# Gates: the weighted one-hot columns of eight tokens are shared between VectorE, GpSimd and ScalarE

## The reference

```python
s, i = lax.top_k(scores, PEER_TOPK)                  # 16 of 128 keys, two halves, 8 heads
cand_s = s[..., 0, :, None] + s[..., 1, None, :]
top_s, sel = lax.top_k(cand_s, PEER_TOPK)            # 16 of 256 pairs
idx = take_along_axis(i0 * 128 + i1, sel)            # one of 16384 experts
gate = softmax(top_s)
act = gelu(einsum('td,ted->te', hx, peer_u[idx]))
out = einsum('te,ted->td', gate * act, peer_v[idx])
```

## Time and profile before

| | us |
|---|---|
| median of 3 runs | 4343.73 (4340.94 to 4347.49) |
| the profiled execution | 4342.6 |
| its span | 4340.8 |
| TensorE busy in the span | 4061.2 |
| VectorE busy | 3090.5 |
| ScalarE busy | 2417.5 |
| GpSimd busy | 95.5 |

### The profile page before, as it was taken

How to read it: one execution, slowest core, us unless ns; L and a number is a source line. 1 busy time by engine, 2 the same in 40 slices (tenths; PEclk the granted TensorE clock), 3 DMA queues, 4 the chain that set the end, 5 groups by cost and what they waited for, 6 DMA issues and landing times.

```text
span 4340.8 us, 84350 instructions
## 1 busy us (share of the span) xinstructions
PE 4061.2 (94%) x30146; PEld 3730.5 (86%) x30146; DVE 3090.5 (71%) x5150; ACT 2417.5 (56%) x4061; POOL 95.5 (2%) x182
## 2 busy tenths in 40 slices
PE   6999997899999999789998999969998999987999
PEld 6899997788889999778888999968887899986887
DVE  6758858867565886787766688598776578768555
ACT  4156658544534665754456666574444466566444
POOL 0000000000000000000000000001000000000000
PEclk9999999999998999999998999999998899999999
DMA  8345551678513555257853555418882255532554
GB/s 283 104 146 175 179 183 54 217 246 289 174 51 127 175 178 181 75 180 250 285 179 120 167 178 180 155 47 298 284 288 106 93 167 176 179 121 68 193 193 155
DMA packets 203625, 748.66 MB, mean 172 GB/s; under 512 B 22704, under 2 KB 23856, under 8 KB 202192
## 3 DMA queue, kind: packets, MB, share of 16 engines
q1 hardware_dynamic: 178416, 646.51, 44.4%
q0 software_dynamic: 25056, 100.15, 7.5%
HBM read 745.52 MB, written 1.05 MB: 172 GB/s over the span
## 4 chain that ended last, share of the span: by engine, by line
PE 83%; DVE 10%; issue 3%; ACT 3%; DMA 1%; DVEq 1%; SPq 0%; ACTq 0%
PE ps L1925 15%; PE ps L1926 14%; PE ps L1932 14%; PE ps L2368 11%; PE ps L2371 11%; PE ps L2375 11%; DVE t_lo L1766 3%; PE ps L2073 2%; DVE arena L1785 2%; DVE oh L1774 2%; PE ps L1946 1%; ACT t_hi L632 1%; DMA raw<-w_tiles 1%; PE ps L2326 1%; PE ps L2217 1%
## 5 line engine op out<-in xcount | busy, mean ns | idle before, releaser
L1108 DVE TENSOR_TENSOR t_lo<-raw,t_hi 128x1024 fp32r<-128x1024 f32 x1180 | 1445.8, 1226 | 1038.2 <-ACT t_hi L632 1017.6
L632 ACT CAST t_hi<-raw 128x1024 fp32r<-128x1024 f32 x1180 | 1237.9, 1050 | 1527.5 <-PE ps L1932 755.5
L1925 PE MATMUL ps<-h_hi,t_hi 128*128 128x256 f32 x5344 | 1349.6, 289 | 42.6 <-DVE h_lo L1240 20.3
L1926 PE MATMUL ps<-h_lo,t_hi 128*128 128x256 f32 x5344 | 1327.6, 285 | 0.0
L1925 PEld LDWEIGHTS ps<-h_hi,t_hi 128*128 128x128 f32 x5344 | 1035.4, 194 | 66.8 <-issue 43.6
L1926 PEld LDWEIGHTS ps<-h_lo,t_hi 128*128 128x128 f32 x5344 | 1038.8, 194 | 0.8 <-issue 0.5
L1932 PE MATMUL ps<-h_hi,t_lo 128*128 128x256 f32 x5240 | 735.2, 283 | 0.0
L1932 PEld LDWEIGHTS ps<-h_hi,t_lo 128*128 128x128 f32 x5240 | 676.3, 192 | 0.0
L2368 PE MATMUL ps<-t_hi,h_hi 128*128 128x512 f32 x2048 | 548.8, 390 | 9.3 <-DVE h_lo L1816 9.3
L2371 PE MATMUL ps<-t_hi,h_lo 128*128 128x512 f32 x2048 | 549.2, 390 | 0.0
L2375 PE MATMUL ps<-t_lo,h_hi 128*128 128x512 f32 x2048 | 548.5, 390 | 0.0
(11 more groups left out here) (284 smaller groups left out, 2961.9 us busy)
## 6 DMA issues: line engine op xcount, KB each, us to landing
raw<-u_tiles SPq DMA_DIRECT2D x512, 512.0 KB, 3.3
raw<-v_tiles SPq DMA_DIRECT2D x512, 512.0 KB, 4.2
raw<-w_tiles SPq DMA_DIRECT2D x188, 512.0 KB, 3.6
oh<-w_tiles POOLq DMA_DIRECT2D x160, 512.0 KB, 4.8
arena<-w_tiles SPq DMA_DIRECT2D x16, 512.0 KB, 3.7
arena<-keys_t POOLq DMA_DIRECT2D x4, 1024.0 KB, 5.0
arena<-mla_w POOLq DMA_DIRECT2D x1, 4096.0 KB, 15.0
arena<-lora POOLq DMA_DIRECT2D x2, 1280.0 KB, 8.8
```

What stands on the lines that cost most here:

```text
L632: act.copy(t_hi[:, j % SPL, :], raw[:, j % RAW, :]).then_inc(hi_done, 1)
L1108: tts(t_lo[:, j % SPL, :], raw[:, j % RAW, :], t_hi[:, j % SPL, :].bitcast(F32), ALU.subtract).then_inc(lo_done, 1)
L1925: mm(o, hi[:, c, :], h_hi[:, c, :], start=(c == 0), stop=False)
L1926: mm(o, hi[:, c, :], h_lo[:, c, :], start=False, stop=False)
```

## The change

A third semaphore, `pooled`, and a function for GpSimd, `middle_hots`, are added. GpSimd makes the columns of tokens 2 and 3 of each octet with the same operation that VectorE uses; VectorE makes those of tokens 0 and 1 only; ScalarE's four stay as they are. TensorE does the products in three groups, 2, 2 and 4, with a wait ahead of each. The results are the same numbers in the same places.

```diff
--- before.py
+++ after.py
@@ -138,6 +138,7 @@
 HSPLIT = {"ffn0": 3, "ffn1": 6, "ffn2": 9, "ffn3": 13, "wo": 11}
 
 EB = 4
+POOL_FROM, POOL_TO = 2, 4
 GATE_BANKS = [6, 0]
 LRU_BANKS = [2, 4, 6, 2]
 POOL_BANKS = [6, 7, 2, 3]
@@ -502,6 +503,7 @@
         hot = sem("hot")
         away_done = sem("away_done")
         weighted = sem("weighted")
+        pooled = sem("pooled")
         gates_t = sem("gates_t")
         gated = sem("gated")
         wah = sem("wah")
@@ -586,6 +588,19 @@
                     tile = 8 * FOLD_ORDER[l][t // 8] + t % 8
                     pool.dma_start(fold_bufs[t % 2], w_tiles[first + tile]).then_inc(ada_in[t % 2], 16)
 
+            def middle_hots(l):
+
+                n = T // 8
+                pool.wait_ge(sel_ready, TT * (l + 1))
+                for m in range(n):
+                    if m >= 2:
+                        pool.wait_ge(gates_t, n * l + m - 1)
+                    for q in range(POOL_FROM, POOL_TO):
+                        t = 8 * m + q
+                        ins = pool.tensor_scalar(hot_cols[m % 2][:, q, :], iota, sel[:, 1, t:t + 1], sel[:, 2, t:t + 1],
+                                                 ALU.is_equal, ALU.mult)
+                    ins.then_inc(pooled, 1)
+
             for l in range(4):
                 if l:
                     if l == 2:
@@ -614,6 +629,7 @@
 
                 pool.wait_ge(h_split, DC * HSPLIT[f"ffn{l}"])
                 pool.dma_start(tk["keys"], keys_t[l]).then_inc(keys_in, 16)
+                middle_hots(l)
                 if l < 3:
                     fetch_late(l + 1)
 
@@ -1768,7 +1784,7 @@
 
                 def columns(m, b):
 
-                    for q in range(4):
+                    for q in range(POOL_FROM):
                         col = lambda w: sel[:, w, bass.ds(m * 8 + q, 1)] if not isinstance(m, int) \
                             else sel[:, w, 8 * m + q:8 * m + q + 1]
                         ins = ts(hot_cols[b][:, q, :], iota, col(1), col(2), ALU.is_equal, ALU.mult)
@@ -2340,18 +2356,19 @@
 
                 def gate(b):
 
-                    for half, made in enumerate((hot, weighted)):
+                    for made, qs in ((hot, range(POOL_FROM)), (pooled, range(POOL_FROM, POOL_TO)),
+                                     (weighted, range(POOL_TO, 8))):
                         seen(made)
-                        o = ps[:, GATE_BANKS[b] + half, :].rearrange("p (e t) -> p e t", t=4)
-                        for q in range(4):
-                            ins = mm(o[:, :, q], hot_rows(l, b)[:, 4 * half + q, :].bitcast(F32),
-                                     hot_cols[b][:, 4 * half + q, :], start=True, stop=True)
+                        for q in qs:
+                            o = ps[:, GATE_BANKS[b] + q // 4, :].rearrange("p (e t) -> p e t", t=4)
+                            ins = mm(o[:, :, q % 4], hot_rows(l, b)[:, q, :].bitcast(F32),
+                                     hot_cols[b][:, q, :], start=True, stop=True)
                     ins.then_inc(gates_t, 1)
 
                 gate(0)
                 pe.wait_ge(taken, TAKEN[f"u{l}"] + KEYS)
                 gate(1)
-                with seen.loop(T // 16 - 1, {hot: 2, weighted: 2, gated: 2}):
+                with seen.loop(T // 16 - 1, {hot: 2, pooled: 2, weighted: 2, gated: 2}):
                     for b in range(2):
                         seen(gated)
                         gate(b)
```

## The result

The changed kernel takes 4292.5 us (median of 4 runs, 4286.2 to 4295.5) against 4343.0 us before: a ratio of 0.9885, 95% interval 0.9874 to 0.9897, that is 50.5 us less. In a second session on one chip it took 4285.8 us against 4342.8, 0.9872 (0.9857 to 0.9887).

What follows compares the result with a forecast made beforehand. VectorE was taken to bound the gate stages at 3.29 us an octet, ScalarE next at 2.85. Four layers gain 45.3 us: 4342.6 - 45.3 = 4297.3, plus 1.1 to the median, 4298 us; range at 8 in 10, 4290 to 4385.

Steps and rivals of the forecast that it cites:

- VectorE bounds, a column is worth 0.255 us, ScalarE's 2.85 us is next: Gate loop: without two VectorE columns, the octet falls from 3.29 us to ScalarE's 2.85 us, not 2.78.
- The end of the stage: First layer's last octets: weights, cast, subtraction, then last gate at 775.5 instead of 786.85, 11.3 us gained.
- thirty cycles on: First layer: octet 31's weights start 30 x 2.853 us after octet 1's at 686.12, at 771.7.
- GpSimd's price: GpSimd's columns: 0.48 us each, 0.96 us a pair, with 0.20 and 1.61 us a pair as ends.
- What an overlap costs: Gate loop: where GpSimd's pair meets VectorE's rows or columns, VectorE would be held; beside the gate multiply it would not.
- A: Rival, gate loop: GpSimd starts between rows and columns, columns wait for the pair; cycle 3.74 us, total 4398; chance 0.24.
- B: Rival, gate loop: pair outlasts the gate multiply and holds the rows; at 0.70 us each, cycle 3.14, total 4326; chance 0.12.
- C: Rival, gate loop: GpSimd at its ceiling, 1.61 us a pair, holds the rows; cycle 3.35 us, 4351 or more; chance 0.10.
- B's formula: Gate loop cycle: 2.78 us plus the pair plus 0.10 to start, less the 1.14 us gate multiply.
- the condition on which the forecast rested: Gate loop: GpSimd's 0.96 us pair runs beside the 1.14 us gate multiply and is over before the one-hot rows begin.
- the alignment protects the kernel: Gate loop: pair and gate multiply wait for the same event, so any interference would have to fall outside that gate.

Runs made afterwards that it cites:

- e9: Changed kernel with ScalarE making three columns of an octet and nobody the fourth, whose gates are left out; gate stage 87.15 us, whole 4284.5 us.
- e5: Changed kernel with one column of an octet for GpSimd instead of two and three for VectorE; gate stage 94.87 us, whole 4319.9 us.
- e2: Changed kernel with three columns of an octet for GpSimd and three for ScalarE; gate stage 98.89 us, whole 4332.6 us.
- e4: Changed kernel with GpSimd making each of its two columns twice from the third octet on; third layer's stage 122.6 us, whole 4430.5 us.
- e7: Changed kernel with three columns each for GpSimd and ScalarE, and the rows' keys in PSUM; gate stage 86.62 us, whole 4280.7 us.
- e6: Changed kernel with three columns for GpSimd and three for ScalarE in odd octets only; gate stage 86.86 us, whole 4276.1 us.
- e10: Changed kernel with one VectorE column, GpSimd three and four in turn, ScalarE four and three, rows' keys in PSUM; gate stage 84.51 us, whole 4275.5 us.

## Why the prediction was right, and where it was not

The forecast was 4298 us and 45.3 us won; 4292.5 us and 50.5 came.

- *VectorE bounds, a column is worth 0.255 us, ScalarE's 2.85 us is next.* Right. The cycle is 2.85 us, ScalarE never idles in it, VectorE waits for 0.08 us (0.07 said). Shown by e9, which takes work from ScalarE alone, and by e5 for the size of a column (its cycles are 3.04 and 3.09 us in turn against 3.29 before: 0.25 us, and 0.20 where the columns meet GpSimd).
- *The end of the stage.* Its links hold: the subtraction follows the cast by 1.08 us (773.54 to 774.62), and the gate follows that by 1.13. The term that was mis-sized is "thirty cycles on": octet 30's weights start at 770.47, 29 cycles behind octet 1's (687.81), but octet 31's follow directly at 772.00, since there are no more distances to make. That cycle is 1.53 us, not 2.85. I had the code's order in front of me and counted a distance that isn't there. It makes 88.7 us of the 90.0 predicted, 1.3 us in each layer, 5 us in all, which is what was missing.
- *GpSimd's price.* 0.48 us was taken between ends of 0.10 and 0.81; it is 0.78 to 0.79, next to the upper end. The pair is 1.56 us and reaches into the rows; the prediction had it over before they begin.
- *What an overlap costs.* The prediction made it VectorE that would pay, in A, B and C alike. By B's formula the real pair would have given 2.78 + 1.56 + 0.10 - 1.14 = 3.30 us an octet, as much as before and no gain at all; with the 0.35 us by which the pair really reached into the rows it would have been 3.13. It was 2.85. e2 and e4 show mostly GpSimd paying instead, and by much only beside the rows. Since GpSimd has nearly two cycles for its columns, a held instruction costs nothing until its list is longer than the cycle. So the bound, the cycle and the place of the pair were right, but the condition on which the forecast rested, a pair over before the rows, was not met. That the rows were not held was luck in this sense: the second GpSimd instruction begins at 717.19, the rows 0.43 us later, and a hold shows only up to 0.30 us (below).
- *That the alignment protects the kernel.* The pair does run beside the gate multiply, but e9 shows that it need not: there it starts with the columns at 720.27 and ends at 721.94, and the rows start at 721.95.
- *The Trainium skill.* The page "SBUF — State Buffer", section "Who interferes with whom", says that a VectorE instruction with two SBUF inputs contends with a GpSimd one that reads SBUF. e2 against e7 agrees, 98.89 against 86.62 us. It also says that the later of the two waits for the other's whole instruction. That holds for GpSimd behind the rows (1.90 us instead of 0.79). For VectorE behind GpSimd it does not: the rows at 717.62 began 0.43 us into a GpSimd instruction of 0.79 and were not held at all. The fast one-input form and GpSimd, which the page lets block each other for a whole instruction, cost each other some 0.06 and 0.1 us (e5, e9).
- *How long GpSimd holds VectorE.* The kept traces have VectorE instructions with two SBUF inputs of 128x1024 (the rows, and the subtractions into `t_lo` before the gates) that begin while a GpSimd instruction runs. Their lengths, by how long GpSimd had been running:

| VectorE began after | 0.08 us | 0.13 | 0.15 | 0.17 | 0.21 | 0.28 | 0.30 and more |
|---|---|---|---|---|---|---|---|
| its length, us | 1.43 | 1.38 | 1.37 | 1.34 | 1.30 | 1.23 | 1.22 |
| found in | e2, e4, e6 | e4 | changed kernel, e2, e4, e5, e6, e9 | e4 | e4 | e2, e4, e6 | changed kernel, e2, e4, e6 to e10 |

Up to 0.28 us, beginning and length of a held one add up to the same, 1.51 to 1.52 us from GpSimd's start: the usual 1.22 and 0.30. So GpSimd holds such an instruction for the first 0.30 us of its own 0.79, and after that no more. Where GpSimd had run for less than some 0.14 us it goes either way: in many such cases, as in e6 with 0.05 us, VectorE keeps its 1.22 us and GpSimd takes 1.84. In e7 the subtraction at 602.42 began 0.05 us ahead of a GpSimd instruction by the profile and was still the one to wait, 1.56 us. The columns fit the same 0.30 us where it was looked at: e9's second column begins 0.24 us after GpSimd and takes 0.39 us instead of 0.34. What GpSimd does in that part of its instruction no run here shows.

## What to carry to other kernels

When work is taken from the bounding engine, the gain ends at the next engine's own pace: read that pace where it waits for nobody, and count its instructions to the very last turn of the loop, where one may be missing. An engine that gets two cycles' notice for its part may be slow and even held up and still cost nothing, until its list is longer than the cycle. One column more (e2) then took back 10.2 of the 12.6 us won in a stage. If GpSimd works beside VectorE, look for VectorE's instructions with two SBUF inputs, and put one of the inputs in PSUM where it lies there anyway.

## What the runs showed that I had not expected

- GpSimd's tensor_scalar of 128x128 takes 0.78 us a piece, start to start, against 0.255 on VectorE. ScalarE needs two activations for a column, 0.71 us together (2.85 / 4).
- The two engines hold each other very unequally. A GpSimd instruction that begins beside a 128x1024 one of VectorE with two SBUF inputs waits for its end, and its 0.79 us become 1.4 to 1.9. The reverse hold ends 0.30 us after GpSimd's start, so VectorE loses 0.2 us as a rule at most (0.34 in e7). With one input in PSUM GpSimd is not held any more, by the rows of e7 as little as by the gate multiply.
- A stretch that no kernel here changes takes 954.8 to 964.0 us, with a granted TensorE clock of 0.980 to 0.972. That is as much as the last improvements are worth.
